# Head norms of an mLSTM layer: averages in four 32-column groups of TensorE, spread to all partitions by transfers

## The reference, cut to what matters

```python
h = jax.nn.sigmoid(o_pre) * hs                      # per head, 256 features
mu = jnp.mean(h, axis=-1, keepdims=True)
var = jnp.mean(jnp.square(h - mu), axis=-1, keepdims=True)
hn = ((h - mu) * lax.rsqrt(var + EPS)) * g_hn
y = hn + skip * xc
y_mix = y * jax.nn.silu(zg)
```

## Time and profile before

| what | value |
|---|---|
| median of 3 runs | 1785.59 us (1785.54 to 1785.86) |
| the profiled execution | 1785.21 us, span 1783.4 us |
| PE busy | 1752.8 us, 98% of the span |
| DVE busy | 850.1 us, 48% |
| ACT busy | 620.0 us, 35% |
| POOL busy | 460.0 us, 26% |
| matmuls of L1315 (both averages of 4 heads) | 48 instructions, 15.2 us busy |

### The profile page before, as it was taken

How to read it: one execution, slowest core, us unless ns; L and a number is a source line. 1 busy time by engine, 2 the same in 40 slices (tenths; PEclk the granted TensorE clock), 3 DMA queues, 4 the chain that set the end, 5 groups by cost and what they waited for, 6 DMA issues and landing times.

```text
span 1783.4 us, 22466 instructions
## 1 busy us (share of the span) xinstructions
PE 1752.8 (98%) x8302; PEld 1372.6 (77%) x8302; DVE 850.1 (48%) x1792; ACT 620.0 (35%) x1504; POOL 460.0 (26%) x511
## 2 busy tenths in 40 slices
PE   8999999999999999999999999999999999999998
PEld 4577765888888888747558888888888888779573
DVE  0444422785666556451332543354435444776613
ACT  1411234654565244311311133423332333843311
POOL 0151100335222012400003552254326443223000
PEclk9999999999999999999999999999999999999999
DMA  8311111245655245541121012223132434844412
GB/s 270 133 60 66 65 44 43 60 159 168 204 168 164 83 98 152 186 144 48 56 74 49 27 46 87 74 67 106 43 113 72 142 114 133 273 144 148 155 69 96
DMA packets 148807, 196.21 MB, mean 110 GB/s; under 512 B 19068, under 2 KB 107900, under 8 KB 148563
## 3 DMA queue, kind: packets, MB, share of 16 engines
q1 hardware_dynamic: 140580, 174.65, 31.1%
q10 hardware_dynamic: 8118, 20.14, 3.0%
HBM read 156.97 MB, written 37.85 MB: 109 GB/s over the span
## 4 chain that ended last, share of the span: by engine, by line
PE 88%; DVE 6%; ACT 3%; DMA 1%; issue 1%; POOL 0%; SPq 0%; ACTq 0%; DVEq 0%
PE PS L3173 48%; PE PS L2208 11%; PE PS L2252 4%; PE PS L375 3%; PE PS L1995 3%; PE PS L539 3%; PE PS L287 2%; PE PS L2031 2%; PE PS L2006 2%; PE PS L2028 1%; DVE WK L708 1%; PE PS L901 1%; PE PS L894 1%; PE PS L1315 1%; PE PS L2220 1%
## 5 line engine op out<-in xcount | busy, mean ns | idle before, releaser
L3173 PE MATMUL PS<-HT,RING 128*128 128x258 f32 (+2 forms) x1776 | 444.4, 381 | 2.6 <-ACT WK L3263 2.1
L3173 PEld LDWEIGHTS PS<-HT,RING 128*128 128x128 f32 x1776 | 329.1, 190 | 48.8 <-ACT WK L3263 2.9
L3263 ACT ACTIVATE BIG<-PS 128x256 f32<-128x256 f32 (+2 forms) x140 | 53.7, 383 | 355.4 <-PE PS L3173 355.0
L3173 PE MATMUL PS<-BIG,RING 128*128 128x258 f32 (+1 forms) x656 | 159.8, 382 | 1.3 <-DVE BIG L3359 1.3
L2208 PE MATMUL PS<-BIG 128*128 128x512 f32 x328 | 147.7, 597 | 0.5 <-DVE BIG L3370 0.5
L3173 PEld LDWEIGHTS PS<-BIG,RING 128*128 128x128 f32 x656 | 122.9, 190 | 19.9 <-DVE BIG L3359 2.1
L2208 PEld LDWEIGHTS PS<-BIG 128*128 128x128 f32 x328 | 60.3, 190 | 69.8 <-issue 68.7
L3173 PE MATMUL PS<-BIG,WK 128*128 128x258 f32 (+1 forms) x448 | 112.4, 382 | 1.0 <-DVE BIG L3359 1.0
L3173 PE MATMUL PS<-HT,CST 128*128 128x256 f32 (+2 forms) x432 | 110.4, 382 | 1.4 <-DVE BIG L3364 1.3
L3173 PEld LDWEIGHTS PS<-BIG,WK 128*128 128x128 f32 x448 | 83.3, 190 | 13.4 <-DVE BIG L3359 1.4
L3173 PEld LDWEIGHTS PS<-HT,CST 128*128 128x128 f32 x432 | 79.4, 190 | 13.4 <-DVE BIG L3364 3.0
(11 more groups left out here) (398 smaller groups left out, 3117.9 us busy)
## 6 DMA issues: line engine op xcount, KB each, us to landing
RING<-in_w_in_a SPq DMA_DIRECT2D x14, 1024.0 KB, 6.1
WK<-in_cache_mem_kv SPq DMA_DIRECT2D x56, 256.0 KB, 5.6
RING<-in_w_kv_b SPq DMA_DIRECT2D x12, 1024.0 KB, 5.3
RING<-in_w_in_b SPq DMA_DIRECT2D x12, 1024.0 KB, 5.5
WK<-in_cache_win SPq DMA_DIRECT2D x40, 256.0 KB, 4.8
RING<-in_w_mkv SPq DMA_DIRECT2D x16, 512.0 KB, 5.1
BIG<-in_x_prompt SPq DMA_DIRECT2D x16, 512.0 KB, 3.3
BIG<-sample_query SPq DMA_DIRECT2D x28, 256.0 KB, 6.0
```

Of the source, the lines that this page charges most:

```text
L3173: last = nc.tensor.matmul(PS[:, bank, 0:mid - lo], weight_block(u // 2, s, k), h_block(layer_of(u), u % 2, t, k), start=(k == 0 and j not ...
L3263: nc.scalar.activation(part(u, n2 if j == 0 else n1, lo, mid), PS[:, banks(u)[0], 0:mid - lo], ACT.Copy).then_inc(sig("projections_copied" ...
```

## The change

For heads 0, 1 and 2 an average is no longer one 128-column matrix times 1032 tokens. The tokens are cut into four quarters of 258 (`QUARTER`), and each quarter goes through 32 columns of the array of its own: four matmuls with a 128 x 32 matrix, whose outputs lie in partitions 0 to 31, 32 to 63, 64 to 95 and 96 to 127 of one PSUM bank. ACT copies (or takes Ln and Exp of) a strip of 258 columns, writes rows 0, 32, 64, 96 of it, which are the four quarters, to a row in DRAM, and reads that row back to all 128 partitions into `ROOT`. DVE takes the mean, and the root, from `ROOT`. The slots of the later steps move. Head 3 stays as it was.

```diff
+        avg_rows_d = dram("head_averages", [6, W])
+        SPREAD = 3
-            job(f"mean{h}", "dve")
+            job(f"mean{h}", "act" if h < SPREAD else "dve")
-        VAR = [x + 16 for x in GATE]
+        VAR = [x + (21 if h < SPREAD else 16) for h, x in enumerate(GATE)]
+        QUARTER = W // 4
@@ layer_a_sp
-                    if x == GATE[h - 2] + 26:
+                    if x == GATE[h - 2] + 32:
                         sp.wait_ge(sig("y_ready").sem, 2 * h - 3)
                         load_xc(sp, h)
@@ average
+            if h < SPREAD:
+                for g in range(4):
+                    last = nc.tensor.matmul(PS[32 * g:32 * (g + 1), 3, 0:QUARTER], avg_h[:, 0:32],
+                                            big(HELD[h][0], g * QUARTER, (g + 1) * QUARTER), start=True, stop=True)
@@ new functions of ACT
+        def save_average(act, h, var):
+            act.wait_ge(*(sig("root_ready").sem, h + 2) if var else read_of(f"mean{h}"))
+            act.dma_start(avg_rows_d[2 * h + var].rearrange("(g n) -> g n", g=4),
+                          ROOT[0:P:32, 0:QUARTER]).then_inc(average_saved(h, var)[0], 16)
+        def spread_average(act, h, var):
+            act.wait_ge(*average_saved(h, var))
+            act.dma_start(ROOT, avg_rows_d[2 * h + var].partition_broadcast(P)).then_inc(average_spread(h, var)[0], 16)
+        def mean_strip(act, h):
+            act.wait_ge(job_done.sem, done(f"mean{h}"))
+            if h > 0:
+                act.wait_ge(sig("y_ready").sem, 2 * h - 1)
+            nc.scalar.activation(ROOT[:, 0:QUARTER], PS[:, 3, 0:QUARTER], ACT.Copy).then_inc(job_read["act"].up(), 1)
+            save_average(act, h, 0)
@@ root_log, root_exp: for h < SPREAD on ROOT[:, 0:QUARTER]; root_exp then calls save_average(act, h, 1)
@@ layer_a_act
-                    if x == GATE[h] + 12:
+                    if x == GATE[h] + (17 if h < SPREAD else 12):
                         squares_act(act, h)
-                    if x == GATE[h] + 17:
+                    if x == VAR[h] + 1:
                         root_log(act, h)
-                    if x == GATE[h] + 18:
+                    if x == (VAR[h] + 1 if h < SPREAD else VAR[h] + 2):
                         root_exp(act, h)
+                    if h < SPREAD:
+                        if x == MEAN[h] + 1:
+                            mean_strip(act, h)
+                        if x == MEAN[h] + 3:
+                            spread_average(act, h, 0)
+                        if x == VAR[h] + 3:
+                            spread_average(act, h, 1)
@@ head_dve
+            centre, summed, norm = (15, 19, 27) if h < SPREAD else (10, 14, 20)
-            if n in (10, 11):
+            if n in (centre, centre + 1):
...
+                if h < SPREAD:
+                    dve.wait_ge(*average_spread(h, 0))
+                    ins = nc.vector.tensor_tensor(y, y, ROOT, ALU.subtract)
-            if n == 14:
+            if n == summed:
-            if n in (20, 21):
+            if n in (norm, norm + 1):
...
+                dve.wait_ge(*(average_spread(h, 1) if h < SPREAD else (sig("root_ready").sem, h + 2)))
-            if n in (22, 24):
-                e = (n - 22) // 2
+            if n in (norm + 2, norm + 4):
+                e = (n - norm - 2) // 2
-            n = x - GATED_3 if h == 3 else n - 25
+            n = x - GATED_3 if h == 3 else n - 32
```

More of the change, by code:

```diff
@@ L1307, in average @@
         def average(pe, name, h, summed):
-            pe.wait_ge(sig(summed).sem, h + 1)
+            pe.wait_ge(sig(summed).sem, 2 * h + 1 if name[0] == "m" else h + 1)
             if name == "mean0":
@@ L1313, in average, with average_saved, average_spread @@
                 pe.wait_ge(*read_of(f"mean{h}" if name[0] == "v" else f"var{h - 1}"))
-            for b in range(3):
-                last = nc.tensor.matmul(AVERAGED[:, b, :], avg_h, big(HELD[h][0], b * SEG, (b + 1) * SEG),
-                                        start=True, stop=True)
-            last.then_inc(job_done.up(), 1)
+            if h < SPREAD:
+                for g in range(4):
+                    last = nc.tensor.matmul(PS[32 * g:32 * (g + 1), 3, 0:QUARTER], avg_h[:, 0:32],
+                                            big(HELD[h][0], g * QUARTER, (g + 1) * QUARTER), start=True, stop=True)
+            else:
+                for b in range(3):
+                    last = nc.tensor.matmul(AVERAGED[:, b, :], avg_h, big(HELD[h][0], b * SEG, (b + 1) * SEG),
+                                            start=True, stop=True)
+            last.then_inc(job_done.up(), 1)
+        def average_saved(h, var):
+            return sig("scratch_saved").sem, 80 + 16 * (2 * h + var + 1)
+        def average_spread(h, var):
+            return sig("rows0_broadcast").sem, 16 * 3 + 16 * (2 * h + var + 1)
+        def save_average(act, h, var):
[11 more added lines that the diff above has]
+            save_average(act, h, 0)
         def woven_a_pe(pe, x):
@@ L1373, in squares_act @@
         def squares_act(act, h):
-            act.wait_ge(*read_of(f"mean{h}"))
+            act.wait_ge(*((sig("values_summed").sem, 2 * h + 2) if h < SPREAD else read_of(f"mean{h}")))
             nc.scalar.activation(tiles2(HELD[h]), tiles2((6 * h, 6 * h + 1)), ACT.Square).then_inc(sig("squares").up(), 1)
@@ L1379, in root_log @@
             act.wait_ge(job_done.sem, done(f"var{h}"))
-            if h > 0:
+            if h < SPREAD:
+                nc.scalar.activation(ROOT[:, 0:QUARTER], PS[:, 3, 0:QUARTER], ACT.Ln,
+                                     bias=EPSC).then_inc(job_read["act"].up(), 1)
+            else:
                 act.wait_ge(sig("y_ready").sem, 2 * h - 1)
-            nc.scalar.activation(seg3(ROOT), AVERAGED, ACT.Ln, bias=EPSC).then_inc(job_read["act"].up(), 1)
+                nc.scalar.activation(seg3(ROOT), AVERAGED, ACT.Ln, bias=EPSC).then_inc(job_read["act"].up(), 1)
         def root_exp(act, h):
             act.wait_ge(*read_of(f"var{h}"))
-            nc.scalar.activation(ROOT, ROOT, ACT.Exp, scale=-0.5).then_inc(sig("root_ready").up(), 1)
+            root = ROOT[:, 0:QUARTER] if h < SPREAD else ROOT
+            nc.scalar.activation(root, root, ACT.Exp, scale=-0.5).then_inc(sig("root_ready").up(), 1)
+            if h < SPREAD:
+                save_average(act, h, 1)
         def gate_act(act, u):
@@ L1465, in head_dve @@
                                         ALU.add).then_inc(sig("values_summed").up(), 1)
-            if n in (10, 11):
-                e = n - 10
-                dve.wait_ge(job_done.sem, done(f"mean{h}"))
-                ins = nc.vector.tensor_tensor(seg3(big(6 * h + e)), seg3(big(6 * h + e)), AVERAGED, ALU.subtract)
+            centre, summed, norm = (15, 19, 27) if h < SPREAD else (10, 14, 20)
+            if n in (centre, centre + 1):
+                e = n - centre
+                y = big(6 * h + e)
+                if h < SPREAD:
+                    dve.wait_ge(*average_spread(h, 0))
+                    ins = nc.vector.tensor_tensor(y, y, ROOT, ALU.subtract)
+                else:
+                    dve.wait_ge(job_done.sem, done(f"mean{h}"))
+                    ins = nc.vector.tensor_tensor(seg3(y), seg3(y), AVERAGED, ALU.subtract)
                 if e == 1:
-                    ins.then_inc(job_read["dve"].up(), 1)
-            if n == 14:
+                    ins.then_inc((sig("values_summed") if h < SPREAD else job_read["dve"]).up(), 1)
+            if n == summed:
                 dve.wait_ge(sig("squares").sem, h + 1)
@@ L1475, in head_dve @@
                                         ALU.add).then_inc(sig("squares_summed").up(), 1)
-            if n in (20, 21):
-                y, j = big(6 * h + n - 20), 2 * h + n - 20
-                dve.wait_ge(sig("root_ready").sem, h + 2)
+            if n in (norm, norm + 1):
+                y, j = big(6 * h + n - norm), 2 * h + n - norm
+                dve.wait_ge(*(average_spread(h, 1) if h < SPREAD else (sig("root_ready").sem, h + 2)))
                 nc.vector.scalar_tensor_tensor(out=y, in0=y, scalar=vec(ROW_GHN, j), in1=ROOT,
                                                op0=ALU.mult, op1=ALU.mult).then_inc(step.up(), 1)
-            if n in (22, 24):
-                e = (n - 22) // 2
+            if n in (norm + 2, norm + 4):
+                e = (n - norm - 2) // 2
                 y, j = big(6 * h + e), 2 * h + e
```

## The result

The changed kernel takes 1795.6 us (median of 6 runs, 1794.8 to 1798.5) against 1785.5 for the kernel before (6 runs beside it): 10.1 us slower, a ratio of 1.0062 with a 95% interval of 1.0052 to 1.0072. I had forecast 1797.5, in a range of 1791.5 to 1807.

A forecast was written before the change was run, and what follows sets the result against it. PE, 88% of the chain that ended last, was taken to bound the kernel. Waits of 18.4 us less 6.3 saved gave 12.1 onto the profiled 1785.2: 1797.3, taken as 1797.5 for the runs' median; range 1791.5 to 1807.

The forecast's parts named there:

- PE's part: Averages of heads 0 to 2 on PE: 0.68 us each instead of 1.73, saving 1.05 us, six times 6.3 us.
- The rival of groups in turn: The four column groups of an average run one after another on PE: saving 0, 1803.8 us; chance 0.04.
- The mean's detour: Mean's strip through DRAM and back before product 24: just in time, cost nothing, bound 2 us.
- The variance's detour: Root's way through DRAM to DVE's norm and the sum for product 38: PE waits 4.4 us there in head 0.
- T: The end of product 28 of head 0, from which the times of the root's steps are counted in us.
- the rival of a faster kernel: Root's broadcast lands by T + 7.2, so product 38 finds its sum: 1779.2 us at best; chance 0.07.
- "Nearly nothing" at product 33: ACT's copy of product 30 ends at T + 7.0, due at product 33, T + 6.9: nearly no wait.
- The second wait: PE at product 41: DVE has 7.2 us of work in three slots of 5.2, so PE waits 2.0 more.
- Loss: PE's waits in heads 0 to 2 together: 3 x 6.4 - 0.8 = 18.4 us.
- gain: PE time saved by the six cheaper averages of heads 0 to 2: 6.3 us.
- the two large waits: PE waiting for DVE's sums at products 38 (4.4 us) and 41 (2.0 us), repeated in heads 1 and 2.
- The clock's rival: PE's clock falls behind the waits of 4.4 us, 1.8 us a head on top: 1803 us; chance 0.21.

The follow-up runs named there:

- The last run: Changed kernel with norm, skip and other steps in later slots, and the mean's strip copied into the head's own free tile: 1779.3 us against 1785.6 for the kernel before.

## Why the prediction was right, point by point

- **PE's part** was sized 1.05 us an average, and is 0.96 in the run with the groups alone. The groups run side by side, as the earlier trace rows had it; switching in and out costs 0.34 us (0.77 less the 0.43 that the columns need at 0.84 ns each) and not 0.25. The rival of groups in turn is out.
- **The mean's detour costs nothing** held: no wait of PE before product 33 of head 0, and none at the products behind the centring of heads 1 and 2. The two waits of 0.3 us at their variance bursts, for the squares' sum (L1528), were not forecast; the run with the slots alone has them too (L1479, 0.6 us), so they are not the transfer's.
- **The variance's detour.** ACT's part was right within 0.3 us (T + 7.4 for 7.1). The landing was 3.5 us in head 0 and not 4.5. DVE's work behind it was 7.4 us in heads 0 and 2 and not 8.4, since norm and skip took 1.29 each, where the rows that I had picked were 1.43 to 1.57. The rows that I had picked run beside a product on POOL; the second skip, a few us later, runs beside none and takes 1.28 (both from the kernel before):

```profile
474.42 2.65 POOL L1167 TENSOR_TENSOR WK<-TRIG 128x256 f32<-128x256 f32 x2 [6.22 <-ACT WK L1182]
```

```profile
479.26 1.28 DVE L1486 SCALAR_TENSOR_TENSOR BIG<-WK,VEC,BIG 128x1032 f32<-128x1032 f32 x1
```

  In the profiles of both kernels between 440 and 640 us every such step of DVE on 1032 columns that takes over 1.30 us overlaps a product on POOL, and those that overlap none take 1.22 to 1.29; but some that overlap one take no longer either. I had named this as a possibility under the rival of a faster kernel. No run here changes POOL's work, so the cause is not shown.

  So product 38 waited 1.9 to 3.7 us, 7.8 in the three heads where I had 13.2. In head 1 the save took 2.5 us (I had 1.4), so the broadcast came later, and DVE's work was 8.3.
- **"Nearly nothing" at product 33** was wrong by 0.6 us a head: the save's issue took 0.50 us of ACT and not 0.33, and the copy of product 30 came just after its time.
- **The second wait** was sized 2.0, 2.0 and 1.2. It was 1.9 in head 0 and 0.4 in both others. In head 1 the half clock gave DVE the time to catch up; in head 2 there are no states, and DVE's work between the two sums took 5.9 us.
- **Loss** 15.6 for 18.4, **gain** 5.0 for 6.3 (two variance slots also held a wait of 0.3 for the squares' sum): 10.6 for 12.1. The mechanism and the places of the two large waits held; the landing, DVE's chain and the second wait were each taken too long. That the total came so close is partly luck. Counted from start to start, products 38 and 41 lost some 6.5 us less than the forecast's 18.4, and 3.7 us came in that it had put at nothing: 1.9 at product 33 and 1.8 by the half clock in head 1.
- **The clock's rival** (0.21) came true in one head of three in the profiled execution. By the Trainium skill (TensorE: Matmul & The Clock Gate, Part 1) an idle array is put back to half clock; the trace agrees for the wait of 3.7 us and shows nothing of it for those of 1.9 and 2.1. In the run with the norm later a wait of 3.1 us was enough.
- **The rival of a faster kernel** hung on the landing at T + 7.2; it was at T + 10.9. The last run shows that the gain could be had, in another order.

## What to carry to other kernels

When a result takes a detour, count two things from the place where it comes back: how long the detour is, and what now stands in the engine's list between it and the next thing that the bounding engine asks for. Here six cheaper averages (5.8 us) were lost to steps that moved seven slots down and met the next head's. The remedy was no faster transfer, but later consumers and a buffer that breaks the tie to the head before. And when you price a step from a row of the trace, look at what ran beside it: the same skip step stood there at 1.57 and at 1.28 us.

## What the runs showed of the hardware

- A wait of PE costs more than its row: product 38 of head 0 starts 3.81 us after product 37, which is 2.07 more than a slot, for a wait shown as 1.91, and the product itself lasts 1.85 in place of 1.74. That is some 0.27 us for this wait; the other waits of that timeline without the half clock show the same 0.1 in the product behind them.
- A burst of eight 32-column instructions between wide matmuls takes 0.77 us of PE, of which 0.43 are its columns at 0.84 ns each (an estimate from the earlier trace rows).
- The issue of the save (four rows of 1 KB from partitions 0, 32, 64, 96) holds ACT 0.50 us (0.59 at most), that of the broadcast of 516 KB 0.32 (0.35 at most).
- The clock fell 3.8 us after PE's last matmul (545.8 to 549.6) in head 1 of the changed kernel, and 4.9 us after it (613.4 to 618.3) in head 2 of the run with the broadcast twice, so the rows give no one delay. The product at half clock took 3.53 us for 1.74.
- Steps of DVE on 1032 columns (SBUF to SBUF) that overlap no step of POOL took 1.22 to 1.29 us (12 of them in the kernel before, 31 in the changed one, between 440 and 640 us); all that took over 1.30 (1.32 to 1.77) overlap one. No run tests whether POOL is the cause.
